# Attention in a two-layer trunk kernel: the next group's maxima turned and its first scores issued ahead of the old group's last values, queries split two groups ahead

## The reference

```python
def attn_probs(s, sink):
    if sink is None:
        return jax.nn.softmax(s, axis=-1)
    m = jnp.maximum(jnp.max(s, axis=-1, keepdims=True), sk)
    e = jnp.exp(s - m)
    return e / (jnp.sum(e, axis=-1, keepdims=True) + jnp.exp(sk - m))
...
# layer 0: every latent query sees 256 cached context keys and all 512 latent keys, no sink
o = blocked_attention(qh, jnp.concatenate([kc, kh], axis=2), jnp.concatenate([vc, vh], axis=2))
# layer 1: 256 cached keys and the latent keys at most 128 away, with a sink logit per head
o = banded_window_attention(qh, kh, vh, kc, vc, sink)
# in both: the 128 context queries see the 128 context keys alone
```

## Time and profile before

| | us |
|---|---|
| median of three runs | 1883.13 |
| lowest, highest | 1880.34, 1886.09 |
| profiled execution | 1881.52 |
| its span, first to last instruction | 1879.8 |
| mean granted TensorE clock, of full speed | 0.958 |
| TensorE busy | 1708.3 (91%) |
| VectorE busy | 1150.6 (61%) |
| ScalarE busy | 639.4 (34%) |
| GpSimd busy | 260.1 (14%) |

### The profile page before, as it was taken

How to read it: one execution, slowest core, us unless ns; L and a number is a source line. 1 busy time by engine, 2 the same in 40 slices (tenths; PEclk the granted TensorE clock), 3 DMA queues, 4 the chain that set the end, 5 groups by cost and what they waited for, 6 DMA issues and landing times.

```text
span 1879.8 us, 29748 instructions
## 1 busy us (share of the span) xinstructions
PE 1708.3 (91%) x11829; PEld 1584.2 (84%) x11829; DVE 1150.6 (61%) x1488; ACT 639.4 (34%) x769; POOL 260.1 (14%) x263
## 2 busy tenths in 40 slices
PE   0499889879999999998898989869999999999997
PEld 0499845779999999998796659669999999999997
DVE  7986457886466667567664663455565665655653
ACT  2212255233221221122333442434444444444441
POOL 3010101330000000003001123040110110110100
PEclk9999999889999999999898989979999999999998
DMA  9153100223334444443210001355765665665652
GB/s 361 61 174 123 48 1 0 90 90 120 115 123 156 149 143 158 148 141 113 68 61 10 0 1 68 137 181 180 228 206 172 231 212 181 224 205 185 221 196 62
DMA packets 45260, 251.12 MB, mean 134 GB/s; under 512 B 5472, under 2 KB 6128, under 8 KB 23824
## 3 DMA queue, kind: packets, MB, share of 16 engines
q1 hardware_dynamic: 28176, 192.14, 28.5%
q0 software_dynamic: 16448, 57.88, 10.6%
q10 hardware_dynamic: 576, 0.26, 0.0%
HBM read 236.60 MB, written 13.72 MB: 133 GB/s over the span
## 4 chain that ended last, share of the span: by engine, by line
PE 79%; DVE 9%; issue 6%; ACT 3%; POOL 2%; DMA 1%; SPq 0%; ACTq 0%; DVEq 0%; POOLq 0%
PE pp L625 55%; PE popr L625 5%; PE pm L625 5%; PE popr L810 4%; DVE dump L1286 3%; PE pp L764 2%; PE pp L913 1%; DVE tmpA L1319 1%; PE pm L790 1%; PE popr L807 1%; DVE h_lo L1331 1%; DVE spread L1480 1%; PE pm L793 1%; DVE tmpB L1313 1%; PE pm L869 1%
## 5 line engine op out<-in xcount | busy, mean ns | idle before, releaser
L1643 DVE TENSOR_TENSOR w_lo<-raw,w_hi 128x2048 fp32r<-128x2048 f32 x108 | 247.3, 2291 | 180.0 <-ACT w_hi L1194 180.0
L625 PE MATMUL pp<-g_hi,w_hi 128*128 128x192 f32 x1152 | 317.7, 276 | 6.2 <-DVE tmpB L1681 4.1
L625 PE MATMUL pp<-h_hi,w_hi 128*128 128x320 f32 x1152 | 272.3, 318 | 54.3 <-DVE h_lo L1331 42.2
L625 PE MATMUL pp<-g_lo,w_hi 128*128 128x192 f32 x1152 | 317.4, 276 | 0.0
L625 PE MATMUL pp<-g_hi,w_lo 128*128 128x192 f32 x1152 | 317.2, 275 | 0.0
L625 PE MATMUL pp<-h_lo,w_hi 128*128 128x320 f32 x1152 | 266.6, 313 | 0.0
L625 PE MATMUL pp<-h_hi,w_lo 128*128 128x320 f32 x1152 | 266.0, 312 | 0.0
L625 PEld LDWEIGHTS pp<-h_hi,w_hi 128*128 128x128 f32 x1152 | 196.6, 192 | 62.0 <-issue 61.1
L625 PEld LDWEIGHTS pp<-g_hi,w_hi 128*128 128x128 f32 x1152 | 223.4, 194 | 6.5 <-DVE w_lo L1643 4.3
L625 PEld LDWEIGHTS pp<-g_lo,w_hi 128*128 128x128 f32 x1152 | 223.3, 194 | 0.0
L625 PEld LDWEIGHTS pp<-g_hi,w_lo 128*128 128x128 f32 x1152 | 223.3, 194 | 0.0
(11 more groups left out here) (238 smaller groups left out, 3077.2 us busy)
## 6 DMA issues: line engine op xcount, KB each, us to landing
raw<-in_ws SPq DMA_DIRECT2D x164, 1024.0 KB, 4.8
modraw<-in_wmod POOLq DMA_DIRECT2D x80, 512.0 KB, 3.7
mod_first<-in_wmod SPq DMA_DIRECT2D x4, 2048.0 KB, 19.6
out_y<-six SPq DMA_DIRECT2D x7, 512.0 KB, 3.4
xT<-in_xT SPq DMA_DIRECT2D x1, 2560.0 KB, 20.1
token_rows<-tok SPq DMA_DIRECT2D x5, 512.0 KB, 2.6
mixer<-in_mixer SPq DMA_DIRECT2D x1, 1473.0 KB, 25.1
scond<-in_cond SPq DMA_DIRECT2D x1, 1024.0 KB, 5.1
```

Source lines behind the costliest of these rows:

```text
L625: ins = mm(out[:, at_bank(lo, hi)], x, y[:, lo:hi], start=f, stop=end)
L1643: V.tensor_tensor(w_lo[b][:], raw[b][:], w_hi[b][:].bitcast(F32), ALU.subtract).then_inc(w_lo_done, 1)
```

## The change

On TensorE, unit u now starts with its first scores already issued by the unit before. For tile k it issues the scores of tile k + 1, then block k of the next unit's maxima (k below 4), then the values of tile k. At k = 4 the next unit's maxima are turned, between the last scores and the values of tile 4; at k = 5 the next unit's first scores are issued ahead of the last values. Unit 8 has one tile: its values come first, then the four maxima, the turn and the first scores of unit 9. The first scores of unit 0 are issued ahead of the loop.

On ScalarE, the maxima row of the next unit comes ahead of the last exponential of u. The next unit's first exponential, behind a wait for a free tile of `probs`, follows, then one half of the queries of unit u + 2, then the copy of the sums of u, then the other half of the queries. The queries of units 0 and 1 are both split ahead of the loop, and the exponential of unit 0's first tile too.

```diff
--- before.py
+++ after.py
@@ -811,21 +811,28 @@
                        ).then_inc(values_done, 1)
 
                 def unit(u, nu, i):
+
                     n = len(attn_tiles(l, u))
-                    for k in range(max(n, 5)):
-                        if k < n:
-                            scores(u, k, i)
-                            if k:
-                                values(u, k - 1, i)
-                        if nu is not None and 1 <= k <= 4:
-                            max_scores(nu, k - 1, i)
-                    if nu is not None:
+                    for k in range(n):
+                        if k + 1 < n:
+                            scores(u, k + 1, i)
+                            if nu is not None and k < 4:
+                                max_scores(nu, k, i)
+                            if nu is not None and k == 4:
+                                turn_max(nu, i)
+                        elif n > 1 and nu is not None:
+                            scores(nu, 0, i)
+                        values(u, k, i)
+                    if n == 1 and nu is not None:
+                        for b in range(4):
+                            max_scores(nu, b, i)
                         turn_max(nu, i)
-                    values(u, n - 1, i)
+                        scores(nu, 0, i)
 
                 for b in range(4):
                     max_scores(0, b, 0)
                 turn_max(0, 0)
+                scores(0, 0, 0)
                 units(pe, unit)
 
             def project_out(l):
@@ -1104,9 +1111,9 @@
                 act.dma_start(newv_d[l], v[:, LAT:TOK]).then_inc(kv_out, 16)
 
             def attention(l):
-                def q_hi(u, i):
-                    for half_rows in (slice(0, HD), slice(HD, P)):
-                        A(blocks(qA[u % 2][half_rows]), unit_q(u, i), ACT.Copy).then_inc(q_hi_done, 1)
+                def q_hi(u, i, halves=(0, 1)):
+                    for x in halves:
+                        A(blocks(qA[u % 2][x * HD:(x + 1) * HD]), unit_q(u, i), ACT.Copy).then_inc(q_hi_done, 1)
 
                 def max_row(u, i):
                     act.wait_ge(max_turned, i * 2 + (UNITS * l + u + 1))
@@ -1132,21 +1139,41 @@
                       ).then_inc(exp_done, 1)
 
                 def unit(u, nu, i):
-                    for k in range(len(attn_tiles(l, u))):
+
+                    n = len(attn_tiles(l, u))
+                    later = None if nu is None or nu + 1 >= UNITS else nu + 1
+
+                    def keep_sums():
+                        act.wait_ge(values_done, i * 12 + (key_step(l, u, n - 1) + 1))
+                        act.wait_ge(out_kept, i * 2 + ((UNITS + 2) * l + u + 1))
+                        A(att_out(u), po, ACT.Copy).then_inc(po_free, 1)
+
+                    def next_first():
+                        act.wait_ge(values_done, i * 12 + (key_step(l, nu) - 2))
+                        exps(nu, 0, i)
+
+                    if n == 1:
+                        keep_sums()
+                        if nu is not None:
+                            max_row(nu, i)
+                            next_first()
+                        return
+                    for k in range(1, n):
+                        if k == n - 1:
+                            max_row(nu, i)
                         exps(u, k, i)
-                        if nu is not None and k == 0:
-                            q_hi(nu, i)
-                    if nu is not None:
-                        max_row(nu, i)
-
-                    last = key_step(l, u, len(attn_tiles(l, u)) - 1)
-                    act.wait_ge(values_done, i * 12 + (last + 1))
-                    act.wait_ge(out_kept, i * 2 + ((UNITS + 2) * l + u + 1))
-                    A(att_out(u), po, ACT.Copy).then_inc(po_free, 1)
+                    next_first()
+                    if later is not None:
+                        q_hi(later, i, (0,))
+                    keep_sums()
+                    if later is not None:
+                        q_hi(later, i, (1,))
 
                 q_hi(0, 0)
                 max_row(0, 0)
                 act.wait_ge(rotated, 5 * l + 5)
+                q_hi(1, 0)
+                exps(0, 0, 0)
                 units(act, unit)
 
             def project_out(l):
```

## The result

The changed kernel takes 1905.45 us (median of four runs, 1903.34 to 1907.8) where the kernel before takes 1883.59 beside it. The ratio is 1.0114, 95% interval 1.0095 to 1.0133: 21.9 us slower. I had forecast 1881.4, a gain of 1.7, with a range of 1875.8 to 1887.4. The time lies outside it, and above the slowest of my rivals (1889.0).

The account below looks back on a forecast made before the run. The prediction took TensorE's order, with its waits at the change of unit, as the bound. Layer 0 at -5.8 and layer 1 at +4.1 gave -1.7, median 1883.1 to 1881.4 us, range 1875.8 to 1887.4.

Parts of the forecast that it names:

- (a): Layer 0, full units: first values wait for the sums' bank; new period 10.4 against 10.9, 0.5 gained for each.
- the clock in layer 1: Layer 1, changes of unit: three clock falls taken instead of the present four, -1.6; bounds none and six.
- Rival 4: Change of unit in layer 1: clock falls in all six, and twice in layer 0; net +5.9, 1889.0; chance 0.10.
- (b): Layer 0's loop: table loads in second and third pass go; with (a), six periods 62.4 against 69.3, -6.9.
- rival 2: Layer 0's loop: the table load stays in it, 1883.7 to 1885.1; chance 0.10.
- (c): Start of layer 0: second unit's query split ahead of the first exponential; +0.2, at most +1.3.
- that of layer 1: Start of layer 1: 1.28 of query split ahead, all at the low clock; +0.8.
- (d): Layer 0's two context units: eighth's turn -0.1; unit 8, values before unit 9's maxima, +1.0, bounds +0.8 and +1.6.
- Layer 1's last two periods: Layer 1's end: eighth turn +0.9, context unit 8 +3.0 as unit 9's maxima come after unit 8's values.
- the waits of 1.21 and 0.80: End of layer 1: the last reciprocals no longer wait for sums, -2.0.
- Rival 3: Layer 0: sums behind the half split eat the whole 0.5, only the table loads go; 1884.4; chance 0.15.
- The signs that I had listed: Changed profile: two fewer loads, layer 0 turns 10.4 apart with 0.3 to 0.4 wait before first values, layer 1 turns 12.2.

Follow-up runs that it names:

- the whole change with both repairs: The changed kernel with the first maxima behind the first values step and two more matmuls ahead of layer 1's denominator: 1882.6 us, 1.0011.

## Why the prediction was wrong

**The step that failed** is in layer 0, (a): "The first values wait for the sums' bank: turn + 3.9." In the changed order the first maxima of the unit after next stand ahead of these values. I had counted them in TensorE's work there (0.34) and didn't ask what they wait for: both halves of a split which ScalarE has just moved to the same place, the second half behind the sums. "Queries split two groups ahead" is no earlier seen from the consumer, because the consumer was moved forward as well. That is +0.87 us for each of six periods (11.27 against 10.4; in the period shown the first values come at turn + 4.75 and the rest takes 6.5, as I had it; with the maxima behind the values they come at turn + 3.66, and the period is 10.63), +0.84 at the eighth turn where I had -0.1, and +0.77 in each full period of layer 1 (12.97 against 12.2).

**The term that was mis-sized** is the clock in layer 1: "I take three: -1.6". It is ten falls where there were four, +10.6 instead of -1.6. Rival 4 had the mechanism and the place but one fall for each unit and no more; in eight of twelve periods the low level lasted twice as long, which no full period of the kernel before shows. My bounds, none and six, were no bounds. The two mistakes hang together: with the first maxima behind the values the same layer has four falls, with work in the wait one. Of the 23.3 us between my -1.7 and the +21.6 of the two attentions, the clock is 12.2 and the longer full periods, at full clock, 9.8 (5.2 in layer 0, 4.6 in layer 1); the rest is the smaller terms.

**What held.** (b) Both table loads went and layer 0's clock stayed up, worth 4.2 us by themselves: rival 2 is dead. The Trainium skill's rule that I had quoted for it ("ScalarE activation tables: per-element evaluation and per-set limits", section "Table sets in the compiler and the runtime", loads placed per block), read as I had read it, a load in each pass, is not what this program shows: its loads followed what the loop was entered with. (c) The start of layer 0 cost 0.2, as said; that of layer 1 0.3 for my 0.8. (d) Unit 8 in layer 0 +0.87 for +1.0. Layer 1's last two periods +4.3 for +3.9, though with other shares, and the waits of 1.21 and 0.80 of the earlier trace rows are gone, -2.0 exactly: the three reciprocals now follow each other without a wait (two of them, from VectorE's timeline):

```profile
1146.31 3.35 DVE L1507 RECIPROCAL spread<-tmpB 64x512 f32<-64x512 f32 x1
...
1150.41 3.35 DVE L1507 RECIPROCAL spread<-tmpB 64x512 f32<-64x512 f32 x1
```

Rival 3 (layer 0's reorder gives nothing, by the sums) did not go far enough: it left the layer 2.8 us shorter by its loads, and the layer came out 0.2 longer. Against the old order without loads (65.15 for six periods) the new one (67.6) loses 2.4, by the maxima's wait and not by the sums. The signs that I had listed would have told the case apart: I had put the wait "before the first values, put down to the copy of the sums", and the trace puts it before L764, to qA.

## What to carry to other kernels

When a producer and its consumer are both moved, write down the order of both engines line by line from the diff and ask of each instruction what it waits for now; a step prepared "two ahead" is worth nothing if its reader moves ahead too. A gap ahead of thin matmuls is priced by the clock first and by its own length second, so look whether the present waits already bring falls, and try filling a wait with matmuls before reordering anything. An operation that looks like overhead (here the one-row pair) may be hiding another engine's work; and a function table's load in a loop may go, as it did here, once the loop is entered with the right table.

## What was new of the hardware

In layer 1 TensorE's clock fell although the engine had not been idle for longer than 1.2 us at a time: behind waits of 0.66 and 1.18 us with full matmuls between them, and in one period shown before the one-row pair had begun. A wait of 1.03 alone between full matmuls brought no fall (six periods of layer 0, in four kernels), the two waits without the pair one in each unit, the two waits with the pair one or two, and 0.48 with the pair two or four in six units. One wait of 0.9 to 1.0 with the pair moved away brought none in six, one of 0.66 with the pair some 1.6 us behind it none in six (the whole change with both repairs), and one of 1.67 or 1.68 in layer 0, at a table load, a fall at one load of two in each of three kernels. A fall cost 1.7 us or, where the clock stayed down twice as long, 3.4. And half a microsecond of useless matmuls in the wait of 0.48 brought it to none in six, in both kernels that had them.
